# Moving weight splitting, search rounds, head loads and memory values in a two-layer attention and ConvGLU trunk

## The reference

```python
for l in range(DEPTH):                      # 2
    proj = rms_norm(h) @ w_in[l]            # q_a, k_a, v_a, indexer, q_b, k_b, v_b
    # A: indexer scores -> top 256 keys of each query -> softmax over these keys
    score = sum_h relu(q_i . k_i) * w_i ; sel = top_k(score, 256)
    out_a = attention(q_a, k_a[sel], v_a[sel])             # 8 heads of 64
    # B: differential attention, 4 heads: softmax(q1 k1) - lam * softmax(q2 k2), times v
    out_b = rms_norm(diff_attention(q_b, k_b, v_b, lam))
    h = h + concat(out_a, out_b) @ w_out[l]
    # memory: 4-head cross-attention into 256 memory tokens
    h = h + softmax(q_mem(h) . k_mem(mem)) v_mem(mem) @ w_o[l]
    # ConvGLU, 2816 features: causal depthwise convolution of width 3 on the gate
    h = h + (silu(conv(gate)) * up) @ w_down[l]
out = rms_norm(h)
```

## Time and the profile before

| | us |
|---|---|
| median of three executions | 3325.55 (3322.5 to 3328.26) |
| profiled execution | 3333.92 |
| its span | 3332.1 |
| PE busy | 3075.4 (92%) |
| DVE busy | 2072.4 (62%) |
| ACT busy | 1522.9 (46%) |
| POOL busy | 827.8 (25%) |

### The profile page before, as it was taken

The page is one execution under the profiler, slowest core; times in us unless marked ns, Lnnn a source line. Parts: engine busy times, 40 slices in busy tenths (PEclk is TensorE's granted clock), DMA queues, the critical chain, the costliest instruction groups (busy, mean ns, idle before and its releaser), DMA issues.

```text
span 3332.1 us, 40063 instructions
## 1 busy us (share of the span) xinstructions
PE 3075.4 (92%) x15032; PEld 2539.9 (76%) x15032; DVE 2072.4 (62%) x3531; ACT 1522.9 (46%) x2554; POOL 827.8 (25%) x422
## 2 busy tenths in 40 slices
PE   7998778899998999999999977879899999999998
PEld 5786765788887888878877866648788778887887
DVE  6558777342448898952447587762334689898234
ACT  5369866432334333321334797673323533334112
POOL 1121046352021222232221100644511112222221
PEclk9998899999999999999999989899999999999999
DMA  5455600331012222252253483003210122223322
GB/s 202 124 139 132 134 7 1 109 93 46 25 51 69 77 76 95 76 164 75 92 148 118 104 172 81 1 30 110 89 38 23 48 76 83 89 76 116 125 72 74
DMA packets 295856, 288.43 MB, mean 87 GB/s; under 512 B 19040, under 2 KB 258144, under 8 KB 295408
## 3 DMA queue, kind: packets, MB, share of 16 engines
q1 hardware_dynamic: 291264, 272.24, 28.6%
q10 hardware_dynamic: 4400, 13.63, 1.2%
HBM read 214.46 MB, written 71.37 MB: 86 GB/s over the span
## 4 chain that ended last, share of the span: by engine, by line
PE 73%; DVE 9%; ACT 7%; DMA 4%; issue 3%; POOL 2%; SPq 2%; ACTq 0%; DVEq 0%; POOLq 0%
PE ps L2036 39%; PE ps L2315 8%; PE ps L2317 8%; PE ps L2316 8%; PE ps L2218 2%; POOL w_lo L805 2%; ACT above L943 2%; SPq L615 2%; DMA raw<-in_w_in 1%; DMA k_b<-qk_spill 1%; DVE p_a L1715 1%; DVE xs_lo L1349 1%; PE ps L2289 1%; PE ps L2210 1%; PE ps L2162 1%
## 5 line engine op out<-in xcount | busy, mean ns | idle before, releaser
L805 POOL TENSOR_TENSOR w_lo<-raw,w_hi 128x512 fp32r<-128x512 f32 (+4 forms) x236 | 461.5, 1967 | 1388.9 <-ACT w_hi L866 1388.8
L2036 PE MATMUL ps<-xs_hi,w_hi 128*128 128x512 f32 (+1 forms) x1728 | 542.8, 396 | 34.2 <-POOL w_lo L805 20.8
L2036 PE MATMUL ps<-xs_lo,w_hi 128*128 128x512 f32 (+1 forms) x1728 | 538.3, 393 | 0.0
L2036 PE MATMUL ps<-xs_hi,w_lo 128*128 128x512 f32 (+1 forms) x1728 | 537.2, 392 | 0.0
L1746 DVE TENSOR_TENSOR h_t<-h_t,ps 128x1024 f32<-128x1024 f32 x96 | 117.2, 1220 | 518.0 <-PE ps L2036 502.8
L866 ACT ACTIVATE w_hi<-raw 128x512 fp32r<-128x512 f32 (+4 forms) x236 | 184.8, 802 | 556.4 <-PE ps L2036 461.8
L2036 PEld LDWEIGHTS ps<-xs_hi,w_hi 128*128 128x128 f32 (+1 forms) x1728 | 323.6, 190 | 113.6 <-issue 33.1
L2036 PEld LDWEIGHTS ps<-xs_lo,w_hi 128*128 128x128 f32 (+1 forms) x1728 | 326.6, 189 | 71.5
L2036 PEld LDWEIGHTS ps<-xs_hi,w_lo 128*128 128x128 f32 (+1 forms) x1728 | 326.0, 189 | 71.5
L828 POOL TENSOR_SCALAR p_a<-p_a,rca 128x1024 f32<-128x1024 f32 (+7 forms) x96 | 186.4, 1949 | 416.3 <-DVE rca L1688 415.1
L1225 ACT ACTIVATE w_hi<-w_sum 128x512 fp32r<-128x512 f32 x210 | 132.6, 632 | 314.5 <-DVE w_sum L1878 237.8
(11 more groups left out here) (350 smaller groups left out, 6413.0 us busy)
## 6 DMA issues: line engine op xcount, KB each, us to landing
raw<-in_w_gu SPq DMA_DIRECT2D x48, 512.0 KB, 4.5
act_spill<-cv SPq DMA_DIRECT2D x44, 512.0 KB, 6.0
raw<-in_w_in SPq DMA_DIRECT2D x32, 512.0 KB, 6.2
raw<-in_w_kv SPq DMA_DIRECT2D x32, 512.0 KB, 3.8
qk_spill<-t_hi SPq DMA_DIRECT2D x24, 512.0 KB, 2.6
qk_spill<-t_lo SPq DMA_DIRECT2D x24, 512.0 KB, 3.2
k_b<-qk_spill SPq DMA_DIRECT2D x32, 384.0 KB
gate_e<-in_w_gu SPq DMA_DIRECT2D x20, 512.0 KB, 4.0
```

The costliest lines, as they stand in the source:

```text
L805: nc.gpsimd.tensor_tensor(w_lo[s][:, w], raw[s][:, w], w_hi[s][:, w].bitcast(f32), ALU.subtract).then_inc(lo_done, 1)
L2036: ins = M(dst[0:c, a:b], w[s][:, k * c:(k + 1) * c], xt[:, a:b], start=(at == 0 and w is w_hi and part == 0), stop=(at == kc - 1 and w is ...
```

## The change

1. POOL makes both parts of the weights of units `qb0` to `out0` (10 to 20): a copy with rounding, then the subtraction. ACT made the high part of them before.
2. 26 rounds of the search stand in the projection and 7 in attention B. The two sets of probes become one, six columns wide: DVE makes one base, one over and one probe where it made two of each; all counts are of keys below the probe.
3. Odd heads of attention B run their query blocks from 7 down to 0. The keys of head 0 are loaded at unit 11 of SP's order instead of unit 15, ahead of its queries, which stay. The load of attention A's queries (`load_sparse(0, 7)`) moves behind the loads of head 2.
4. `MEMORY_AT` sets which memory units follow each output unit: keys in groups of 2, 3, 3 after `out2` to `out4`, values in groups of 2 after `out5` and `out6`, the last four values after `out7`. Before, keys came in pairs after `out2` to `out5` and all eight values after `out7`.
5. The weight sums of the first pair and the four block sums X7 are made on POOL; `taps(0)`, two passes of the convolution over 128x1024, stands on DVE ahead of the low parts of the first blocks instead of behind them.

```diff
+MEMORY_AT = [0, 0, 0, 2, 5, 8, 10, 12, 12]
...
-        if 2 <= m < 6:
-            u += memory[2 * (m - 2):2 * (m - 1)]
-    u += memory[KC:]
+        u += memory[MEMORY_AT[m]:MEMORY_AT[m + 1]]
+    u += memory[MEMORY_AT[KC]:]
...
-ROUNDS[U_AT["vb", (0, 1)]] = ROUNDS[U_AT["vb", (1, 1)]] = 3
-B_STEPS = [h * NB + qb for h in range(B_HEADS) for qb in range(NB // 2)][:33 - sum(ROUNDS.values())]
+for _n in (U_AT["rb", 1], U_AT["vb", (0, 0)], U_AT["vb", (0, 1)], U_AT["vb", (1, 1)], U_AT["qa", 2]):
+    ROUNDS[_n] = 3
+STEPS = [(h, NB - 1 - i if h % 2 else i) for h in range(B_HEADS) for i in range(NB)]
+STEP_AT = {step: u for u, step in enumerate(STEPS)}
+POOL_SPLITS = range(U_AT["qb", 0], N_PROJ + 1)
+B_STEPS = [u for u, (_, qb) in enumerate(STEPS) if qb < NB // 2][:33 - sum(ROUNDS.values())]
...
+                if n == section(U_AT["kb", 2]) + 3:
+                    after(sp, idx_done, len(SEL) * I_HEADS)
+                    wait_spilled(section_tiles(U_AT["kb", 2]))
+                    load_head_keys(0)
                 if n == section(U_AT["qb", 2]) + 2:
-                    after(sp, idx_done, len(SEL) * I_HEADS)
                     wait_spilled(section_tiles(U_AT["qb", 2]))
-                    load_head(0)
+                    load_head_queries(0)
...
+                if g % U in POOL_SPLITS:
+                    pool.wait_ge(w_dma[s], 16 * (g // 2 + 1))
+                    for ks in parts(g % U):
+                        w = slice(ks[0] * c, (ks[-1] + 1) * c)
+                        nc.gpsimd.tensor_copy(w_hi[s][:, w], raw[s][:, w]).then_inc(hi_done, 1)
...
+                        for q in (0, 1, 2, 5):
+                            first_sum(q)
+                        last_blocks()
+                        first_sum(6)
                         gate_up(0)
...
-                    if n < N_PROJ and n != VW_AFTER + 1:
+                    if n + 1 not in POOL_SPLITS and n not in (VW_AFTER + 1, N_PROJ):
                         split_hi(n + 1)
...
-                    m = mark(V.tensor_tensor(over_v[:, :], cnt_v[:, :], need_v[:, :], ALU.is_lt))
-                    after(dve, count_done, len(BY_ACT) * r)
-                    m2 = mark(V.tensor_tensor(over_a[:, :], cnt_a[:, :], need_a[:, :], ALU.is_lt))
-                    dve.wait_ge(dve_step, m)
-                    mark(V.scalar_tensor_tensor(probe_v[:, :], over_v[:, :], -float(2 ** bit), base_v[:, :], ALU.mult, ALU.add))
-                    dve.wait_ge(dve_step, m2)
-                    at["probe"] = mark(V.scalar_tensor_tensor(probe_a[:, :], over_a[:, :], float(2 ** bit), base_a[:, :], ALU.mult, ALU.add))
+                    link(V.tensor_tensor(over[:, :], below[:, :], need[:, :], ALU.is_gt))
+                    at["probe"] = mark(V.scalar_tensor_tensor(probe[:, :], over[:, :], -float(2 ** bit), base_p[:, :], ALU.mult, ALU.add))
...
                 sum_blocks(BLOCKS_THEN[1])
+                taps(0)
                 low_blocks(BLOCKS_THEN[1])
-                product_sum(2)
                 product_lo(2)
                 product_lo(3)
-                taps(0)
```

More of the change, by code:

```diff
@@ L95 @@
 RAW_FIRST = [b for b in BLOCKS if b[0] in ("X1", "X3", "X4")]
-SUM_FIRST = [b for b in BLOCKS if b[0][0] == "X"]
+SUM_FIRST = [b for b in BLOCKS if b[0][0] == "X" and b[0] != "X7"]
 CHUNK_AT = [0, 1, 2, 3] + [8, 9, 10, 11, 4, 5, 6, 7] + [0, 1, 2, 3, 12] + [13, 8, 9, 10, 11]
@@ L147, in b_events @@
     ev = []
-    steps = [divmod(u, NB) for u in range(B_HEADS * NB)]
+    steps = STEPS
     for u in range(len(steps) + 3):
@@ L384, in program @@
         search_at = TAB + 3 * KB
-        (probe_v, base_v, over_v, need_v, cnt_v, probe_a, base_a, over_a, need_a, cnt_a) = (
-            at(n, [P, nv if n[-1] == "v" else nsel - nv], f32, search_at + 32 * k) for k, n in enumerate(
-                ("probe_v", "base_v", "over_v", "need_v", "cnt_v", "probe_a", "base_a", "over_a", "need_a", "cnt_a")))
+        (probe, base_p, over, need, below, keys_n) = (
+            at(n, [P, nsel], f32, search_at + 32 * k) for k, n in enumerate(("probe", "base_p", "over", "need", "below", "keys_n")))
         (top, below_zero, low_scale, low_bias, low) = (
@@ L805, in split_lo, with first_sum, last_blocks @@
                     nc.gpsimd.tensor_tensor(w_lo[s][:, w], raw[s][:, w], w_hi[s][:, w].bitcast(f32), ALU.subtract).then_inc(lo_done, 1)
+            def first_sum(q):
+                dst, (x0, x1, op) = wait_sum_operands(pool, q), sum_operands(q)
+                nc.gpsimd.tensor_tensor(dst, x0, x1, op).then_inc(sum_pool, 1)
+            def last_blocks():
+                for k in range(4):
+                    if k < 3:
+                        after(pool, up_read, 4 + k + 1)
+                    else:
+                        wait_full(pool, ("unit", U_AT["up", 0]))
+                    nc.gpsimd.tensor_tensor(block_at(2, ("X7", k)), h_quarter(4 + k, 0), h_quarter(4 + k, 1), ALU.add).then_inc(x7_done, 1)
             def scale_up(f):
@@ L942, in count_above @@
                     w = (qb + 1) * P
-                    A(signs[:, a:a + w], keys(nv + b), ACT.Sign, bias=probe_a[:, b:b + 1],
-                      accum_out=cnt_a[:, b:b + 1]).then_inc(count_done, 1)
+                    A(signs[:, a:a + w], keys(nv + b), ACT.Sign, scale=-1.0, bias=probe[:, nv + b:nv + b + 1],
+                      accum_out=below[:, nv + b:nv + b + 1]).then_inc(count_done, 1)
                     a += w
@@ L1072, in root_heads @@
                 def root_heads():
-                    for i in range(4, 8):
-                        wait_drained(act, ("V", B_HEADS - 1, i))
+                    for step in STEPS[-4:]:
+                        wait_drained(act, ("V", *step))
                     A(ssb[:, :], ssb[:, :], ACT.Sqrt, scale=1.0 / P, bias=eps[:, 0:1]).then_inc(root_done, 1)
@@ L1122, in _ @@
                         p, half = m
-                        m = 2 * p + half
+                        tail = n - U_AT["out", KC - 1] - 1
                     if kind == "out" and m == 0:
@@ L1138, in _ @@
                             square(NORMS * l + 1, k)
-                    if kind == "vm" and m < 4:
-                        if m == 0:
+                    if kind == "vm" and tail >= 0:
+                        if tail == 0:
                             wait_full(act, ("unit", U_AT["out", KC - 1]))
-                        if m == 3:
+                        if tail == 3:
                             wait_drained(act, ("unit", U_AT["out", KC - 1]))
-                        for k in range(2 * m, 2 * m + 2):
+                        for k in range(2 * tail, 2 * tail + 2):
                             gained(l, G_MQ, k)
-                        if m == 3:
+                        if tail == 3:
                             square(NORMS * l + 1, KC - 1)
@@ L1475, in first_probe @@
                 def first_probe(half):
-                    t = 0.0 if half == 0 else 32768.0
-                    mark(V.memset(probe_v[:, :], t))
-                    at["probe"] = mark(V.memset(probe_a[:, :], 0.5 - t))
+                    at["probe"] = mark(V.memset(probe[:, :], (0.0 if half == 0 else 32768.0) - 0.5))
                 def offer():
```

175 lines of the change are left out of this document (91 added, 84 removed).

## The result

The changed kernel took 3302.95 us (median of four executions, 3298.63 to 3306.23), the kernel before 3324.03 beside it: a ratio of 0.9942, with a 95% interval of 0.992 to 0.9963. It is faster, by 21 us and not by the 60 that were forecast, and 3303 lies outside the range of 3238 to 3298. A second set of executions gave 0.9911 (0.9894 to 0.9929).

What follows compares the result with a forecast made beforehand. PE, busy 92% of the span, was taken as the bound, so gains come only where it idles. Layer 0's 28.4 and layer 1's 31.8 us make 60.2, from 3325.55 to 3265 us; range 3238 to 3298.

Steps and rivals of the forecast that it cites:

- Projection: Second half of the projection: PE's waits for POOL's `w_lo` go, 6.5 of 8.1 us in layer 0, 4.5 of 7.3 in layer 1.
- Unhindered, 26 rounds end ahead of the last unit: Projection: with three more search rounds of 3.08 us, the search still finishes before the last unit.
- part of which ACT's counts cover: Projection: POOL's subtraction holds DVE's small search rows up to 2 us a unit, partly hidden behind ACT's counts.
- contention: Rival: POOL rows hold DVE's small search rows, projection and products gain nothing; 3285 to 3298 us, chance 0.2.
- the 26 rounds now set the end of the projection: Rival, nothing moves: the search ends the projection and gives attention B's 9.2 us back; 3310 or 3325 us, chance 0.07.
- The copy holds DVE as the subtraction does: Rival, slower: in the projection DVE's chain rows stand 6.0 us per unit; 73 us slower, 3398, chance 0.08.
- Attention B: Three rounds fewer, no `k_b` wait, and turned heads with first copies partly covered: 15.4 us in layer 0, 18.9 in layer 1.
- What `load_sparse` then delays is attention A's queries: Attention B: moving that load behind head 2's loads delays only queries needed some 70 us later.
- the `k_b` wait: Attention B: PE's wait for a head's keys goes, 3.0 us in layer 0 and 6.9 in layer 1.
- Memory: Last eight memory values: half of PE's 8.9 us stall remains, key groups give some 1.5 back; 3 us gained per layer.
- Products: First seven products: DVE loses nine rows, 6.1 us; gain 2 of 8.0 us idle in layer 0, 3.4 of 9.2 in layer 1.
- Attention A's start: Attention B's last step becomes a block of 128 keys instead of 1024, shortening the tail: 1.5 and 2 us.

Runs made afterwards that it cites:

- the one-input row: Changed kernel, but POOL makes the low weight parts of units 10 to 20 by multiplying raw by zero instead of the subtraction: 3286.08 us, 0.9861 of before.
- the run with late keys: Changed kernel with attention A's queries behind head 3's loads and high parts on ACT, but head 0's keys loaded at unit 15: 3284.69 us, 0.988 of before.

## Why the prediction was wrong

**Projection, forecast -6.5 and -4.5 us, measured -0.1 and +1.0.** The step read the gain from PE's idle time, and PE did lose all of it: its projection ends 11.3 us earlier. The step that failed is "Unhindered, 26 rounds end ahead of the last unit", and "part of which ACT's counts cover" with it. The search was no passenger of the projection: its chain of counts on ACT and small rows on DVE ended with PE's work before (last `over_a` at 301.8, PE's end at 302.3), and now ends 11 us behind it: the first exponential follows PE's end by 14.3 us instead of 3.1. First, there was no slack. I had counted a round by ACT's three counts, 3.08 us, but on the chain it is 3.74 from one `over` to the next, so three more are 11.2 us and not 9.2, just what PE gained. With the one-input row the exponential follows PE's end (292.3) by 5.1 us; take off the 3.9 us for which rows are still held there, and by this estimate 26 rounds end about with PE, not a unit ahead of it. With the high parts on ACT it is 9.0, and no row is held. Second, on a chain without slack held rows count in full, and I had given them 1.6 us of the 8.1. They cost 7.9 us against the one-input row. Against ACT's high parts the chain ends 4.5 us later; the three traces with copies and subtractions on POOL have the first exponential at 303.4 to 305.8, the five with the high parts on ACT and the early keys at 298.6 to 301.7. I had this as a rival twice, as contention (0.2) and as "the 26 rounds now set the end of the projection" (0.07); both happened together.

**The copies on POOL.** I priced them between 1.06 and 3.6 us and called both ends hidden. The mean was 1.13 and the shortest 1.04, as fast as ACT's row of 1.06. The Trainium skill (GPSIMD Engine Reference, "Engine selection") says that GpSimd's one-input work is roughly at line rate; the copy agrees, the multiplication of 2.77 us does not. "The copy holds DVE as the subtraction does", which I gave 0.08 as a rival, is true of the single row, for 1 us and not for 6.0 a unit: two small rows were held by copies for 1.4 us in all. I had taken as evidence against it, but that is a multiplication, which held nothing there. What I didn't see is what the copy does to the time of the subtraction behind it. The gaps of the earlier trace rows were put down to ACT's queue, but the run with late keys shows that they came from the DMAs in front of the raw loads, and with those moved ACT could keep the high parts.

**Attention B, forecast -15.4 and -18.9, measured -3.6 and -5.6.** "What `load_sparse` then delays is attention A's queries" is the step that failed. I followed the DMAs past head 2 and stopped; they now stand in front of head 3's, and cost 13.1 us in layer 0 and 13.7 in layer 1. Without them attention B is 16.7 us shorter than before (121.9 against 138.6) and 18.9 in layer 1 (122.4 against 141.3), the sum that I had. Its terms are another matter: the rounds are worth 9.4 for 9.2 forecast, the turned heads 7.9 for 3.2, and these two already exceed 16.7, so that nothing is left for the `k_b` wait that I had counted as 3.0. In layer 1 they are 9.2 and 7.4 of 18.9, which leaves 2.3 for a wait of 6.9. What took the rest of that wait's price wasn't tried.

**Memory, forecast -3 and -3, measured -1.2 and -1.5.** The last value units' waits for `w_lo` fell from 7.1 us to 5.0 in layer 0 and not by half, and PE's matmuls of the next output tile wait 1.5 us behind each group of three keys, as priced at "some 1.5", twice instead of once. Together 8.0 us for 7.1, with 1.0 for 1.8 at the first memory query: the idle time that the step was to remove only moved. What fell is PE's busy time in the stretch, 117.1 to 116.1; why, no run shows.

**Products, forecast -2 and -3.4, measured -3.8 and -3.7** with all that follows in the layer, of which -3.1 and -3.1 in the products themselves. The size came out by luck, for its source is wrong: it was to be PE's idle time, and this fell by 0.5 us in layer 0 (three gaps of 8.0 us became one of 7.43) and by 0.3 in layer 1 (9.2 to 8.9). The nine rows did leave DVE, but POOL's rows held what stayed:

```profile
1005.90 5.85 DVE L1900 SCALAR_TENSOR_TENSOR xs_raw<-h_t,packs,xs_raw 128x512 f32<-128x512 f32 x4
...
1007.77 7.33 POOL L863 TENSOR_TENSOR xs_raw<-h_t 128x512 f32<-128x512 f32 x4
1011.68 2.30 DVE L1943 SCALAR_TENSOR_TENSOR cv<-gs,packs,cv 128x1024 f32<-128x1024 f32 x1
```

A row of X7 takes POOL 1.8 us and not the 1.3 that I had estimated, and DVE's rows in the kernel before took 1.28 us for this `cv` and 0.7 for each `xs_raw`, where they now take 2.30 and 1.5. The other 2.6 us of the 3.1 are PE's busy time in the products (404.7 to 402.2); in layer 0 the lower clock was granted for 6.8 us instead of 10.2, in layer 1 for 10.2 as before, so the clock explains part of it at most.

**Attention A's start, forecast -1.5 and -2, measured -2.4 and -6.9.** The step took the gain from B's last block, now of 128 keys. That isn't it: with every head from small to large again the stretch is 179.7 and 179.5 us, and 181.2 and 180.1 in the same kernel with turned heads. It lasts 178 to 182 us in all changed kernels and 183 to 185 before; what shortens it, and why layer 1 gains more, stays open. So does what the single probe set is worth by itself, which was not tried.

## What to carry to other kernels

Idle time of the busiest engine is a bound on the gain only if nothing else ends with that engine: before filling a gap, look for the second chain that ends at the same place, here the search, and take the boundary between stages at the first instruction that needs both. When a group of DMAs is moved, name the next group behind its new place and when that one is needed, not only the one that it was in front of. And work handed to GpSimd should be costed by when it runs against VectorE's short dependent rows, because a single small row that is held costs the other engines in the chain the rest of GpSimd's row.

## What was not expected of the hardware

The same ten GpSimd subtractions of 2.4 us held no VectorE row of the search when they started behind ScalarE's pass (`over` 166 ns), and held rows of six columns to a mean of 620 ns when they started behind a GpSimd copy. A held row of six columns ends with the GpSimd row, be it a subtraction or a copy of one input (0.79 us for 0.17 under a copy of 1.04). But a GpSimd multiplication by a constant, 2.77 us long, held rows only in its first 1.06 us, and rows that started later in it took 0.17. And GpSimd's copy with rounding of 128x1024 takes 1.04 us where its multiplication by a constant takes 2.77 and its multiplication by a column 3.46.
